# Expert selection two groups ahead, in four parts between the row products, in a two-block network on one Trainium2 core

## The reference, cut to what matters

```
def block(xb):                                        # 128 tokens at a time
    q = (xb @ w_q).reshape(n, 8, 2, 128)
    s = einsum('nhpc,pkc->nhpk', q, sk)               # 2 x 128 key scores per head
    sv, si = top_k(s, 16)
    cand = sv[:, :, 0, :, None] + sv[:, :, 1, None, :]
    cand_id = si[:, :, 0, :, None] * 128 + si[:, :, 1, None, :]
    fv, fi = top_k(cand.reshape(n, 8, 256), 16)
    eid = take_along_axis(cand_id.reshape(n, 8, 256), fi)
    gw = softmax(fv)
    u = u_tab[eid]                                    # 16384 x 1024 table
    act = gelu(einsum('nhkd,nd->nhk', u, xb))
    return einsum('nhk,nhkd->nd', gw * act, v_tab[eid])
```

## Time and profile before

| | us |
|---|---|
| median of 3 runs | 3106.19 |
| lowest, highest | 3097.05, 3106.47 |
| the profiled execution, its own time | 3097.9 |
| its span in the trace | 3095.9 |
| busy: PE | 2542.0 (82%) |
| busy: DVE | 1746.6 (56%) |
| busy: POOL | 1095.9 (35%) |
| busy: ACT | 802.0 (26%) |
| experts stage of layer 0, first gather to the last product in `acc` | about 263 to 951 |
| experts stage of layer 1 | about 1125 to 1816 |

### The profile page before, as it was taken

How to read it: one execution, slowest core, us unless ns; L and a number is a source line. 1 busy time by engine, 2 the same in 40 slices (tenths; PEclk the granted TensorE clock), 3 DMA queues, 4 the chain that set the end, 5 groups by cost and what they waited for, 6 DMA issues and landing times.

```text
span 3095.9 us, 29274 instructions
## 1 busy us (share of the span) xinstructions
PE 2542.0 (82%) x10643; PEld 1701.7 (55%) x10643; DVE 1746.6 (56%) x3404; ACT 802.0 (26%) x1430; POOL 1095.9 (35%) x1162
## 2 busy tenths in 40 slices
PE   8968777777788986777777779977789989987898
PEld 7837333222235572222333349863359979875797
DVE  0145676666754256666677535549925545465454
ACT  1112222212121312121122133443223343324332
POOL 0003777777761027777777720026600000000000
PEclk9979988898899998888888889988899999999899
DMA  7417999999994469999999945540035545521353
GB/s 236 136 61 243 409 409 409 405 409 401 409 402 131 125 216 407 409 408 408 406 404 405 403 162 179 204 129 1 14 116 164 196 151 177 201 85 56 123 179 120
DMA packets 322158, 766.83 MB, mean 248 GB/s; under 512 B 22016, under 2 KB 172448, under 8 KB 322016
## 3 DMA queue, kind: packets, MB, share of 16 engines
q0 software_dynamic: 150208, 546.77, 44.9%
q1 hardware_dynamic: 170576, 217.69, 21.6%
q10 hardware_dynamic: 1232, 0.50, 0.1%
HBM read 763.83 MB, written 1.05 MB: 247 GB/s over the span
## 4 chain that ended last, share of the span: by engine, by line
PE 50%; DVE 19%; DMA 13%; POOL 10%; issue 7%; ACT 1%; ACTq 0%; DVEq 0%; POOLq 0%
PE ps L267 29%; PE acc L267 20%; DMA arena<-in_peer_u,arena 12%; POOL arena L1023 10%; DVE arena L988 3%; DVE arena L1636 2%; DVE arena L919 1%; DVE arena L925 1%; DVE arena L921 1%; DVE arena L923 1%; DVE arena L917 1%; PE ps L325 1%; DVE arena L951 1%; DVE arena L1619 1%; DMA arena<-in_peer_v,arena 1%
## 5 line engine op out<-in xcount | busy, mean ns | idle before, releaser
L267 PE MATMUL acc<-arena 128*128 128x512 f32 (+2 forms) x2490 | 1099.2, 598 | 378.6 <-ACT arena L912 277.3
L267 PEld LDWEIGHTS acc<-arena 128*128 128x128 f32 (+1 forms) x2490 | 469.5, 194 | 999.1 <-issue 647.5
L1023 POOL DMA_INDIRECT arena<-in_peer_u,arena x512 | 486.9, 951 | 418.5 <-DVE arena L961 242.0
L1023 POOL DMA_INDIRECT arena<-in_peer_v,arena x512 | 482.1, 942 | 207.5 <-issue 127.2
L299 DVE TENSOR_TENSOR lo_ring<-ring,hi_ring 128x2048 fp32r<-128x2048 f32 x132 | 302.1, 2290 | 332.6 <-ACT hi_ring L291 332.3
L988 DVE CUSTOM_DVE_ANT_0 arena<-arena,ps 128x1024 f32<-128x1024 f32 x256 | 306.8, 1220 | 214.4 <-DMA arena<-in_peer_u,arena 213.8
L988 DVE CUSTOM_DVE_ANT_0 arena<-arena,acc 128x1024 f32<-128x1024 f32 x256 | 305.4, 1219 | 190.4 <-DMA arena<-in_peer_u,arena 188.9
L267 PE MATMUL ps<-x_hi,hi_ring 128*128 128x256 f32 x1408 | 401.5, 285 | 11.2 <-DVE x_lo L1204 11.2
L267 PE MATMUL ps<-x_lo,hi_ring 128*128 128x256 f32 x1408 | 401.0, 285 | 0.0
L267 PE MATMUL ps<-x_hi,lo_ring 128*128 128x256 f32 x1408 | 400.8, 285 | 0.0
L291 ACT CAST hi_ring<-ring 128x2048 fp32r<-128x2048 f32 x132 | 250.9, 1902 | 438.5 <-PE ps L267 337.9
(11 more groups left out here) (315 smaller groups left out, 2301.4 us busy)
## 6 DMA issues: line engine op xcount, KB each, us to landing
ring<-in_ffn_w SPq DMA_DIRECT2D x132, 1024.0 KB, 5.5
ring<-in_peer_w_q SPq DMA_DIRECT2D x16, 1024.0 KB, 5.4
ring<-in_mlstm_w_in SPq DMA_DIRECT2D x12, 1024.0 KB, 5.3
arena<-in_peer_u,arena POOLq DMA_INDIRECT x512, 8.7
arena<-in_peer_v,arena POOLq DMA_INDIRECT x512, 8.6
ring<-in_cv_w_in SPq DMA_DIRECT2D x8, 1024.0 KB, 5.5
ring<-in_rglru_w_in SPq DMA_DIRECT2D x8, 768.0 KB, 5.0
ring<-in_w_out SPq DMA_DIRECT2D x5, 1024.0 KB, 4.8
```

The lines of the kernel that those rows point to most:

```text
L267: return pe.matmul(o, l, r, start=first, stop=last)
L1023: pool.indirect_dma_start(ring_[:, g % slots, :], None, table, bass.IndirectOffsetOnAxis(ix[j % 4][:, k:k + 1].bitcast(U32), 0), element_o ...
```

## The change

The selection is cut into four parts: part 0 and part 1 are the `dve_topk` over each set of 128 scores, part 2 the pair sums, the `dve_topk` over them and "nmax", part 3 the row numbers. Group j now carries the selection of group j+2, a part behind each of the products k = 3, 7, 11 and 15 (behind k = 3 the coefficients come first). Group 0 carries two selections: those of groups 1 and 2, a part behind every odd k. There are six lists of row numbers in place of four, at another place of the arena. Each row product is still one instruction, in the same order. The token rows already lie in PSUM before the change.

```diff
+        IX = 6
-        ix = small(23648, 4, PR_K)
+        ix = small(23844, IX, PR_K)
...
-        def dve_select(i, j):
+        def dve_select(i, j, part):
...
+            if part < 2:
+                if t == 0 and part == 0:
+                    dve.wait_ge(act_steps, count_of(f"read ps{i}.{h}"))
+                at = 256 * h + 128 * part
+                dve_topk(sv[b][:, part, :], si_u[b][:, part, :].bitcast(U32), sc[:, t, at:at + 128])
+            elif part == 2:
...
+                if j >= 2:
+                    dve.wait_ge(act_steps, count_of(f"ex {i}.{j - 2}"))
+                dve_topk(fv[b], fi[b].bitcast(U32), cand.rearrange("p a b -> p (a b)"))
...
+            else:
...
-            if j >= 4:
-                dve.wait_ge(pe_steps, count_of(f"v used {PR_K * (NJ * i + j - 4) + PR_K - 1}"))
+                if j >= IX:
+                    dve.wait_ge(pe_steps, count_of(f"v used {PR_K * (NJ * i + j - IX) + PR_K - 1}"))
...
         def dve_peer(i):
-            dve_select(i, 0)
+            for part in range(4):
+                dve_select(i, 0, part)
             for j in range(NJ):
-                dve_dots(i, j, 0, 4)
-                if j:
-                    dve_coef(i, j - 1)
-                dve_dots(i, j, 4, 8)
-                if j + 1 < NJ:
-                    dve_select(i, j + 1)
-                dve_dots(i, j, 8, PR_K)
+                for k in range(PR_K):
+                    dve_dots(i, j, k, k + 1)
+                    if j and k == 3:
+                        dve_coef(i, j - 1)
+                    if j == 0:
+                        if k % 2:
+                            dve_select(i, 1 + k // 8, k % 8 // 2)
+                    elif j + 2 < NJ and k % 4 == 3:
+                        dve_select(i, j + 2, k // 4)
             dve_coef(i, NJ - 1)
...
-                                                  bass.IndirectOffsetOnAxis(ix[j % 4][:, k:k + 1].bitcast(U32), 0),
+                                                  bass.IndirectOffsetOnAxis(ix[j % IX][:, k:k + 1].bitcast(U32), 0),
```

More of the change, by code:

```diff
@@ L926, in dve_topk @@
             dve.wait_ge(dve_steps, VE.n)
-        def dve_select(i, j):
+        def dve_select(i, j, part):
             t, h, b = j // PR_HEADS, j % PR_HEADS, j % 2
[L931 to L958, removed]
-            if j >= 4:
-                dve.wait_ge(pe_steps, count_of(f"v used {PR_K * (NJ * i + j - 4) + PR_K - 1}"))
-            dve.scalar_tensor_tensor(ix[j % 4].bitcast(U32), ids[:, 0, :], float(PR_KEYS), ids[:, 1, :], ALU.mult, ALU.add).then_inc(dve_steps, VE.step(f"ix {i}.{j}"))
-            dve.wait_ge(dve_steps, VE.n)
@@ new lines, in dve_select @@
+            if part < 2:
[4 more added lines that the diff above has]
+            elif part == 2:
+                dve.tensor_scalar(si_f[b][:, 0, :], si_u[b][:, 0, :].bitcast(U32), float(PR_KEYS * i), None, ALU.add).then_inc(dve_steps, VE.step())
+                dve.tensor_copy(si_f[b][:, 1, :], si_u[b][:, 1, :].bitcast(U32)).then_inc(dve_steps, VE.step())
+                dve.tensor_tensor(cand, sv[b][:, 0, :].unsqueeze(2).to_broadcast([P, PR_K, PR_K]),
+                                         sv[b][:, 1, :].unsqueeze(1).to_broadcast([P, PR_K, PR_K]), ALU.add).then_inc(dve_steps, VE.step())
+                dve.wait_ge(dve_steps, VE.n)
+                if j >= 2:
+                    dve.wait_ge(act_steps, count_of(f"ex {i}.{j - 2}"))
+                dve_topk(fv[b], fi[b].bitcast(U32), cand.rearrange("p a b -> p (a b)"))
+                dve.tensor_scalar(nmx[b], fv[b][:, 0:1], -1.0, None, ALU.mult).then_inc(dve_steps, VE.step(f"nmax {i}.{j}"))
+            else:
+                dve.tensor_scalar(ab_u[:, 0, :].bitcast(U32), fi[b].bitcast(U32), 4, None, ALU.logical_shift_right).then_inc(dve_steps, VE.step())
+                dve.tensor_scalar(ab_u[:, 1, :].bitcast(U32), fi[b].bitcast(U32), 15, None, ALU.bitwise_and).then_inc(dve_steps, VE.step())
+                dve.wait_ge(dve_steps, VE.n)
+                dve.tensor_copy(ab_f, ab_u.bitcast(U32)).then_inc(dve_steps, VE.step())
+                dve.wait_ge(dve_steps, VE.n)
+                dve.tensor_tensor(eq, ab_f.rearrange("p a b -> p (a b)").unsqueeze(2).to_broadcast([P, 2 * PR_K, PR_K]),
+                                         iota16[:, :].unsqueeze(1).to_broadcast([P, 2 * PR_K, PR_K]), ALU.is_equal).then_inc(dve_steps, VE.step())
+                dve.wait_ge(dve_steps, VE.n)
+                eq4 = eq.rearrange("p (a b) c -> p a b c", a=2)
+                dve.tensor_tensor(eq4, eq4, si_f[b].unsqueeze(2).to_broadcast([P, 2, PR_K, PR_K]), ALU.mult).then_inc(dve_steps, VE.step())
+                dve.wait_ge(dve_steps, VE.n)
+                dve.tensor_reduce(ids.rearrange("p a b -> p (a b)"), eq, AX, ALU.add).then_inc(dve_steps, VE.step())
+                dve.wait_ge(dve_steps, VE.n)
+                if j >= IX:
+                    dve.wait_ge(pe_steps, count_of(f"v used {PR_K * (NJ * i + j - IX) + PR_K - 1}"))
+                dve.scalar_tensor_tensor(ix[j % IX].bitcast(U32), ids[:, 0, :], float(PR_KEYS), ids[:, 1, :], ALU.mult, ALU.add).then_inc(dve_steps, VE.step(f"ix {i}.{j}"))
+                dve.wait_ge(dve_steps, VE.n)
```

## The result

| | before | after |
|---|---|---|
| median | 3100.31 us (20 runs) | 3106.28 us (20 runs) |
| lowest, highest | 3093.78, 3109.09 | 3100.95, 3108.69 |
| profiled execution, span | 3097.9, 3095.9 | 3104.61, 3102.5 |
| mean granted clock | 0.911 | 0.908 |

The ratio is 1.0015, with an interval of 1.0008 to 1.0022: by the means of the runs 4.6 us slower (by the medians 6.0), where 4.6 us faster was forecast. That is inside the range, and under the 0.3% that was called no change. (One of the 20 runs of the kernel before took 5152.0 us; it is in the median, but not in the line under it nor in the ratio.)

A forecast was written before the change was run, and what follows sets the result against it. The DMA engines were taken as the bound, so only starts gain: -1.8 (layer 0) and -2.8 (layer 1) make -4.6 us, 3093.3 for the profiled execution; with the median 8.3 us over it, 3101.6. Range 3089 to 3113.

The forecast's parts named there:

- What bounds the kernel: Experts stages: DMA engines bound at 409 GB/s, 41.0 us a group of 32 gathers; POOL 3% behind, DVE a third under.
- Instructions: Per layer, none added or removed, no DMA more, less or on another queue: sum 0.
- lists: Six lists of row numbers: the waits on "v used" concern rows long used, sum 0.
- the cut in steady groups: Groups 1 to 15: hold of U slots falls from 9.75 to 3.19 us, gain nothing; coefficients not late, cost 0.
- ACT: Part 2 of selection j+2 waits for ACT's "ex i.j", ready about half a group early, some 20 us: cost 0.
- The schedule of the starts: Group 0, both layers: U(1, 0) some 3.8 us earlier; layer 0 coefficients at 311.7, V(0, 8) at 316.3 after a 5 us hold.
- One sign: Start of layer 0, 280 to 310 us: gather rate above 390 GB/s if the forecast was right.
- The size of the gain: At the starts, missing rate 4.2 us in layer 0, of which 1.8 stays, and 2.8 in layer 1, all staying.
- Rival 3: Group 0: the second selection gives back all the first gained, nothing moves, 3106.2 us; chance 0.15.
- Rival 1: Experts stages: all the missing rate comes back, 12.6 us, to 3093.6 us; chance 0.16.
- Rival 2: Every group: coefficients late behind part 3, 0.9 us lost in each of 30 groups, to 3128.6 us; chance 0.14.
- The rule of the Trainium skill on the shared ports: VectorE using both SBUF ports locks out GpSimd's descriptor writes: 15 us worse if POOL were the bound; sum left unchanged.

## Why the prediction was right or wrong

*What bounds the kernel*: right at 409 GB/s. Groups kept 41.4 us when PE's hold was taken away, and when the selection was moved, cut or both.

*Instructions, lists, the cut in steady groups, ACT*: right, cost 0. The waits for L944 left ACT and nothing came of it. Late in the group the fourth part cost nothing visible.

*The schedule of the starts*: right. "ix 0.1" at 288.04 (forecast 288.05), U(1, 0) at 290.25 (290.0), coefficients at 311.90 (311.7), V(0, 8) at 316.68 after 5.32 us (316.3 after 5), the dip behind it; in layer 1 coefficients at 1175.73 (1174.5), which is 49.2 us after the first gather as forecast, since the stage began 1.2 us later. One sign failed: from 280 to 310 us the rate was 375 GB/s and not above 390.

*The size of the gain*: wrong, and this is the step that failed: "only the rate missing under 409 GB/s can be won", with 4.2 us in layer 0 and 2.8 in layer 1. A rate under the best one was read as idle engines. The DMA share beside it in the earlier trace rows already said 1.00 and 1.04: they were full, in part with small packets of weights. Measured: about 1.7 us won from 280 to 310 us and most of it given back by 330 (-0.8 us in the stage, forecast -1.8), and nothing in layer 1 (+1.1, forecast -2.8). There every forecast of the schedule came true, V(0, 8) "no later than before" among them (54.0 us after the first gather for 54.4), and still nothing was won: with the share at 1.04 there was nothing to win. V(1, 8) was then held 3.81 us (2.46 before). The other half of the step was mis-sized too: V(0, 8) of layer 0, held 5.32 us, landed 5.6 us after its issue, at 322.3, where it had landed at 323.0, 0.7 us won and not 1.8. In place of -4.6 the stages gave +0.3.

*The sign of the total*: +4.6 us by the means. Of the 6.6 us between the two traces 0.3 are in the stages and 4.3 in the untouched second block, which took longer with more time at the lower clock. The long times come in the kernel before too, only less often. All this stands against an error of 0.11% (3 us), seen with the kernel before against itself. I had written that the level at which the median falls counts for more than my sum, and it did; that the change might move that level was not in the sum.

*The rivals.* Rival 3, nothing moves because the second selection gives back what the first gained, is what happened in the stages. Rival 1 had nothing to get back. Rival 2 didn't occur: in layer 0 no steady hold grew over 2.5 us, in layer 1 two did, to 3.8 and 2.7, and the groups kept their length. *The rule of the Trainium skill on the shared ports* (page "SBUF — State Buffer", section "SBUF: two separate sides"): it would have shown as longer issues and a longer group. The page says it of a VectorE instruction in a 2-port mode, which is narrower than my wording. The mean issue is 0.943 us for U and 0.949 for V in the changed kernel's page, 0.951 and 0.942 in that of the kernel before, and the group kept its length; no run here shows a cost.

*Not foreseen*: on chips that gather at 365 GB/s the change wins 0.5%, where I had taken the holds of U slots as free. As these runs show it, they are free while DVE's selection runs through without a stop (9.75 us) and not when it takes 20.4.

## What to carry to other kernels

Before counting a low GB/s as something to win, read the DMA share beside it and the queues under it. Here a share of 1 at a lower rate was another traffic's small packets, and what was issued earlier only changed places with it. A wait that moves to another name when it is removed, with the same group time, was slack. Count the times of a stage from its own start before comparing windows of two traces. And a reordering that is worth nothing on one chip can be worth half a per cent on another whose transfers are slower and whose engines stop now and then: there a long block of work in one piece made holds of up to 7.4 us.

## What the runs showed of the hardware

- Identical gathers (128 rows of 4 KB) pass at 404 to 409 GB/s on some chips and at 356 to 371 on the three others, and the kernel before takes some 3100 or some 3250 us with them.
- On those three, DVE and POOL stop for 2 to 6 us now and then without a releaser in the trace (DVE inside the selection 2.3, 2.3 and 4.6 us). The stops and the lower rate go together, and the runs don't tell which causes which, nor whether something else does that ran beside the program.
- The same instructions behind the stages take 1278 to 1280 us, with 174 to 178 us of them at the lower granted clock, or 1284 to 1285, with 188 to 211. 64 matmuls of them take 27.72 us at a granted clock of 1.00 and 29.41 at 0.94. Nothing in that part was changed.
